# Sample attention over the paged cache: the maximum's chain, the register loads and the exponentials in another order

## The reference, cut to what matters

```python
ckv_past = cache_ckv[j][page_table].reshape(bs, -1, R_KV)      # 8 samples, 4096 rows of 256
kpe_past = cache_kpe[j][page_table].reshape(bs, -1, D_ROPE)    # 8 samples, 4096 rows of 32
sp = (einsum('bqhr,bkr->bhqk', ql, ckv_past) + einsum('bqhd,bkd->bhqk', qp, kpe_past)) * MLA_SCALE
p = softmax(concatenate([sp, s], axis=-1), axis=-1)            # s: the score of the new token itself
o = einsum('bhqk,bkr->bqhr', p[..., :n_past], ckv_past) + einsum('bhqk,bkr->bqhr', p[..., n_past:], ckv)
```

## Time and profile before

| | |
|---|---|
| median of three runs | 3507.61 us |
| the profiled execution | 3497.2 us, its span 3495.1 us |
| busy share of the span | TensorE matmul 85%, VectorE 62%, ScalarE 41%, GpSimd 37% |
| granted TensorE clock, mean | 0.961 |
| sample attention | 1930.4 to 2145.2 us from the span's start |

### The profile page before, as it was taken

One profiled execution on the slowest core, in us unless ns is written; L12 is line 12 of the kernel. 1 busy time (PEld: TensorE's weight loads), 2 busy tenths in 40 slices (PEclk: granted clock), 3 DMA queues, 4 the chain that ended last, 5 costly groups with the idle time before them and its releaser, 6 DMA issues. The chain is left out here.

```text
span 3495.1 us, 34133 instructions
## 1 busy us (share of the span) xinstructions
PE 2962.2 (85%) x10273; PEld 1451.8 (42%) x10273; DVE 2162.7 (62%) x5228; ACT 1420.9 (41%) x4150; POOL 1301.0 (37%) x1112
## 2 busy tenths in 40 slices
PE   8987888888888888887999876888888888888887
PEld 7643333433434433432554544433333444433332
DVE  4873667666677766664262223666766676866765
ACT  3121445444444544443352122444444444543444
POOL 0211544444544444442001010454444444444442
PEclk9988999999999999999999798999999999999999
DMA  4015999999999999998203586999999999999998
GB/s 163 20 61 219 419 422 414 421 421 417 418 407 421 414 421 421 420 419 348 102 1 163 182 313 246 418 421 421 417 422 420 416 407 421 406 421 421 421 421 360
DMA packets 197093, 1213.48 MB, mean 347 GB/s; under 512 B 24527, under 2 KB 46959, under 8 KB 56869
## 3 DMA queue, kind: packets, MB, share of 16 engines
q0 software_dynamic: 154368, 1128.34, 77.9%
q1 hardware_dynamic: 41245, 82.06, 6.5%
q10 hardware_dynamic: 1296, 0.90, 0.1%
HBM read 1207.23 MB, written 4.46 MB: 347 GB/s over the span
## 5 line engine op out<-in xcount | busy, mean ns | idle before, releaser
L1581 PE MATMUL p_acc<-p_rows,p_diag 128*128 128x512 f32 (+1 forms) x4160 | 1976.1, 617 | 406.6 <-ACT p_diag L1184 404.8
L1096 POOL DMA_INDIRECT p_rows<-in_peer_uv,p_ids x1024 | 1217.6, 1189 | 1383.5 <-PE p_acc L1581 1279.5
L1414 DVE CUSTOM_DVE_ANT_0 p_rows<-p_rows,p_x_n 128x1024 f32<-128x1024 f32 x1024 | 1244.5, 1224 | 787.3 <-DMA p_rows<-in_peer_uv,p_ids 784.6
L1581 PEld LDWEIGHTS p_acc<-p_rows,p_diag 128*128 128x128 f32 (+1 forms) x4160 | 755.6, 193 | 1502.7 <-ACT p_diag L1184 780.3
L1178 ACT ACTIVATE p_acts<-p_dots 128x1 f32<-128x1 f32 x1040 | 208.3, 200 | 866.1 <-DVE p_dots L1414 864.1
L1184 ACT ACTIVATE p_diag<-ident,p_gated 128x128 f32<-128x128 f32 x1024 | 411.1, 401 | 33.5
L1180 ACT ACTIVATE p_gated<-p_acts,p_gates 128x1 f32<-128x1 f32 x1024 | 301.6, 295 | 33.2
L1531 PE MATMUL p_q_bank<-p_w_q,p_xT 128*128 128x256 f32 x1024 | 236.2, 384 | 2.2 <-ACT p_xT L1127 2.2
L1531 PEld LDWEIGHTS p_q_bank<-p_w_q,p_xT 128*128 128x128 f32 x1024 | 197.0, 193 | 55.9 <-issue 28.5
L1150 ACT COPY p_q_rows<-p_q_bank 128x256 f32<-128x256 f32 x68 | 25.2, 371 | 353.2 <-PE p_q_bank L1531 353.2
L1623 POOL DMA_INDIRECT smp_past<-in_cache_rows,smp_row_ids x32 | 30.1, 940 | 367.1 <-PE c_ps L2103 228.7
(11 more groups left out here) (408 smaller groups left out, 2489.2 us busy)
## 6 DMA issues: line engine op xcount, KB each, us to landing
d_turned_c<-in_cache_turned SPq DMA_DIRECT2D x128, 144.0 KB
p_w_q<-in_w_q_heads SPq DMA_DIRECT2D x16, 1024.0 KB, 12.8
p_rows<-in_peer_uv,p_ids POOLq DMA_INDIRECT x1024, 13.5
a_w_in<-in_ab_w_in SPq DMA_DIRECT2D x6, 1024.0 KB
a_w_in<-in_ab_w_out SPq DMA_DIRECT2D x1, 4096.0 KB
c_arena<-in_c_w_out SPq DMA_DIRECT2D x1, 4096.0 KB, 12.6
smp_past<-in_c_w_out SPq DMA_DIRECT2D x1, 4096.0 KB
a_w_in<-in_ab_w_in SPq DMA_DIRECT2D x4, 1008.0 KB, 21.0
```

What stands on the lines that cost most here:

```text
L1096: nc.gpsimd.indirect_dma_start(out=rows[:, slot % RING, :], out_offset=None, in_=w[f"peer_uv{layer}"], in_offset=bass.IndirectOffsetOnAxis ...
L1414: nc.vector.tensor_tensor_reduce(rows[:, k % RING, 0:D_MODEL], rows[:, k % RING, 0:D_MODEL], x, 1.0, 0.0, ALU.mult, ALU.add, dots[:, slot ...
L1581: last = nc.tensor.matmul(acc[done % 2][0:n, at], diag[:, slot // GROUP % 4, j, 0:n], rows[:, (slot + j) % RING, D_MODEL + 512 * b:D_MODEL ...
```

## The change

Four edits, all in `latent_sample`:

1. `load_turned` fills all eight registers of a piece first, then waits for `s_ps`, then issues the eight DMAs.
2. The exponential over 1024 scores becomes two over 512 each, each with its own signal and its own column of sums (three columns instead of two); the waits on `e_ready` count halves.
3. TensorE: `fold_heads(b - 2)` goes ahead of group 0, `turn_max(b - 1)` ahead of group 1, `spread_max(b - 1)` ahead of groups 2 and 3.
4. ScalarE: `exps(b - 1)` goes ahead of the copy of group 2. VectorE: `largest(b - 1)` goes ahead of the copy of group 1.

```diff
@@ load_turned (SyncE)
+                starts = [nc.sync.value_load(smp["turned_ids"][0:1, at:at + 1], min_val=0, max_val=w["cache_turned"].shape[0] - 128)
+                          for at in range(KEYS_8 * piece, KEYS_8 * piece + KEYS_8)]
                 if piece >= TURNED_BUFS:
                     sp.wait_ge(s_ps, 2 * ((piece - TURNED_BUFS) // 2 + 1))
-                for k in range(KEYS_8):
-                    at = KEYS_8 * piece + k
-                    row = nc.sync.value_load(smp["turned_ids"][0:1, at:at + 1], min_val=0, max_val=w["cache_turned"].shape[0] - 128)
+                for k, row in enumerate(starts):
                     sp.dma_start(turned_c[:, piece % TURNED_BUFS, k, :], w["cache_turned"][bass.ds(row, 128), :]).then_inc(turned_in[piece % TURNED_BUFS], 16)
@@ exps (ScalarE)
-                nc.scalar.activation(sc[:], s_bank[:, :], ACT.Exp, bias=nbias[:], scale=MLA_SCALE, accum_out=sums[:, 0:1]).then_inc(e_ready, 1)
-                nc.scalar.activation(self_e[:, 0:B], self_s[:, b, :], ACT.Exp, bias=nbias[:], scale=MLA_SCALE, accum_out=sums[:, 1:2]).then_inc(self_e_ready, 1)
+                for half in range(2):
+                    at = slice(KEYS * half, KEYS * half + KEYS)
+                    nc.scalar.activation(sc[:, at], s_bank[:, at], ACT.Exp, bias=nbias[:], scale=MLA_SCALE, accum_out=sums[:, half:half + 1]).then_inc(e_ready, 1)
+                nc.scalar.activation(self_e[:, 0:B], self_s[:, b, :], ACT.Exp, bias=nbias[:], scale=MLA_SCALE, accum_out=sums[:, 2:3]).then_inc(self_e_ready, 1)
@@ order on ScalarE
-                page_out(b, 2)
                 if b:
                     exps(b - 1)
+                page_out(b, 2)
@@ order on VectorE
-                page_out(b, 1)
                 if b:
                     largest(b - 1)
+                page_out(b, 1)
@@ scores, turn_weights (TensorE)
-                    pe.wait_ge(e_ready, b)
+                    pe.wait_ge(e_ready, 2 * b - 1 + half)
-                pe.wait_ge(e_ready, b + 1)
                 for half in range(2):
+                    pe.wait_ge(e_ready, 2 * b + 1 + half)
@@ order on TensorE
+                if b >= 2:
+                    fold_heads(b - 2)
                 turn_pages(b, 0)
                 if b == 0:
                     latent_queries()
-                if b >= 2:
-                    fold_heads(b - 2)
-                turn_pages(b, 1)
...
                 if b:
                     turn_max(b - 1)
+                turn_pages(b, 1)
+                if b:
+                    spread_max(b - 1)
                 turn_pages(b, 2)
                 if b == 0:
                     self_scores()
                 turn_pages(b, 3)
-                if b:
-                    spread_max(b - 1)
                 scores(b, 0)
```

More of the change, by code:

```diff
@@ L2209, in latent_sample @@
         nbias = sb("nbias", [128, 1])
-        sums = sb("sums", [128, 2])
+        sums = sb("sums", [128, 3])
         total = sb("total", [128, 1])
@@ L2220, in latent_sample @@
         o_bank = ctx.enter_context(nc.psum_tensor("d_o", [128, 2 * R_KV], F32))
-        m1_row, bias_col, total_cols = m_bank[0:1, 0:128], m_bank[:, 128:129], m_bank[:, 132:134]
+        m1_row, bias_col, total_cols = m_bank[0:1, 0:128], m_bank[:, 128:129], m_bank[:, 132:135]
         fold_out, self_turned = m_bank[:, 192:192 + 2 * H_C], m_bank[:, 256:384]
```

## The result

The changed kernel takes 3477.5 us, the median of six runs (3476.34 to 3484.32). The kernel before took 3507.28 us in its six (3504.94 to 3509.02). The profiled execution of the changed kernel took 3477.95 us, its span is 3475.9 us.

What follows compares the result with a forecast made beforehand. It took TensorE's waits in sample attention, chiefly for late turned-cache DMAs beside the gather, as the bound; -9.9 + 0.7 - 0.5 + 0.1 - 0.3 = -9.9 us off 3507.6 gave 3497.7 us, range 3487 to 3505.

Steps and rivals of the forecast that it cites:

- the mechanism: SyncE, turned loads: registers loaded before the scores end, eight issues in 4.1 us instead of 9.8, landed about when the gather begins.
- the price of the waits that go: TensorE before the turned half: waits of iterations 3 to 6 go, iteration 2's stays, 14.4 - 4.5 = 9.9 us saved.
- The base: Whole kernel: saving of 9.9 us taken off the median, 3507.6, though the profiled execution was 10.4 us below it.
- What is late next: Per sample, SyncE's 19.4 us and the DMA engines' 18.3 us both fit periods of about 21.5, by 2 to 3 us.
- rival B: Turned-cache wait stays in part, bursts moving slowly or meeting the gather: half remaining gives 3502.6 us, all 3507; chance 0.20.
- Iteration 2: Its turned-cache wait of 4.47 us stays, because SyncE is behind and issues piece 5 under the gather.
- Iteration 1: Scores start at 1967.5 against 1968.04, -0.5 us; piece 3 lands with a cover of 1 us.
- The term of +0.7: Edits 2 to 4, iterations 3 to 6: scores at +8.52 after the gather's start against +8.17, together +0.7 us.
- The held signal (R): TensorE's signal to ScalarE, next the bias, is held until 5.65 us after the gather's start.
- The halves: ScalarE: two exponentials of 512 scores take 2 x 0.59 = 1.18 us, fixed cost 0.07 each.
- A: More than forecast: register loads overlap or held signals come earlier, iteration 2 gains too; 3491, with all 3486 us; chance 0.20.
- C: Slower: TensorE idles longer ahead of the first half, 7.5 us, with slow clock, 12 us; +9.6, 3517 us; chance 0.06.

Runs made afterwards that it cites:

- The burst that starts with the gather: Kernel before with edit 1 alone, pieces from 5 on also waiting for the weighted sum that releases the gather: 3514.42 us, ratio 1.0024.
- the usual execution of before: The kernel before, unchanged, run and profiled once more: 3506.57 us, ratio 1.0001; its profiled execution took 3506.88 us.
- Edit 1 alone: The kernel before with only the new load_turned, eight registers loaded ahead of the wait: 3474.31 us, ratio 0.992.
- the constants: Kernel before with edit 1 alone, fixed rows in place of register loads (wrong keys, same bytes and DMAs): 3464.99 us, ratio 0.9879.
- issues given to GpSimd: Kernel before with edit 1 alone, GpSimd issuing piece 4 and half of each odd piece from 5 on: 3465.53 us, ratio 0.9883.

## Why the prediction was wrong, by its steps

**Edit 1: the mechanism held, its size did not.** What was forecast of SyncE is there. Seven gaps between the issues of piece 3 take 3.61 us, 0.52 each (forecast 0.51); eight loads take 4.4 us (from the last issue of a piece to the first of the next 4.93 us where nothing is waited for; forecast 4.7). That the seven DMAs of the earlier trace rows bear out 0.51 was a slip, though: from the first start to the last end there are six gaps, (3.79 - 0.34) / 6 = 0.575 us. And not every burst is issued within the 4.1 us forecast: pieces 5, 7 and 13 take 4.41, 5.18 and 4.87 us. In iterations 3 to 5 the eight issues still end ahead of the gather's first packets, and the wait is gone. The burst that starts with the gather shows that this is the cause. On that contention the Trainium skill, "DMA: Bandwidth & Descriptors" (Queues, rings and completion order), says that each engine takes its queues in turn, a packet at a time; the nearly equal packet counts of the earlier trace rows agree.

**The failed step is the price of the waits that go, 14.4 - 4.5 = 9.9 us.** It priced the wait of one execution and left the rest of the iteration as it stood in it, 21 to 22 us for iterations 3 to 6. Measured: 17.59 in 3 to 5, and 24.84 in 6. Of iteration 3's 24.1 us, 2.96 was the wait. Another 1.97 us was the late start of the scores (+8.17 against the usual +6.20), and 1.39 us the slow first half behind it (3.31 against 1.92 us). I took both as fixed. They were no part of the normal run: the delay is absent in the usual execution of before, and the slow half followed a wait. In the usual execution the four waits of iterations 3 to 6 are 26.2 us (7.03 + 6.66 + 5.10 + 7.42) and the slow turned halves behind them some 9.8 (3.64 against 1.92 us, and a longer rope part). Together that is the 36.0 us by which these four iterations are longer than four of iteration 7's length. The change took 28.2 of them: iteration 6 kept 7.3, and the four periods are each 0.13 us longer than before without a wait (17.59 against 17.46). Edit 1 alone, in its own trace, took 34.1. An upper bound stood in the rows: iteration 7 does the same work on TensorE in 17.5 us, so the four iterations had about 25 us to lose even in that execution (24.1 + 23.4 + 24.3 + 23.4 - 70). I didn't ask what kept them from it.

**The base.** I saw that the profiled execution was 10.4 us under the median and subtracted its difference from the median. That is right only if the 10 us lie outside the stage. They lay inside it, in the very waits that the change takes away: 225.5 against 214.8 us, with 35.0 against 14.4 us of waits for the turned cache.

**What is late next.** Forecast: SyncE's 19.4 us a sample fit into periods of 21.5. Measured: 17.7 to 18.6 us from one odd piece to the next (2001.63, 2019.97, 2037.62, 2056.24), a bit better, but the periods became 17.59. So SyncE falls behind, by up to a us per sample, until piece 13 meets its gather: 4.80 us of wait and the slow half behind it, 7.3 us. That is rival B's mechanism, in one iteration of four. The DMA engines, forecast at 18.3 us a sample, have hardly more room: in iteration 4 of the changed kernel their share is 1.04, at 397 GB/s, where it was 0.81 in iteration 3 before. A step that shortens a period has to be followed by a second look at everything that was to fit into it.

**Iteration 2** kept its wait, as forecast, and for the reason given; the wait is 8.88 us instead of 4.47, as it was before in the usual execution (8.81).

**Iteration 1.** Forecast a gain of 0.5 us, with a cover of 1 us for piece 3. Piece 3 is issued from 1962.37 to 1966.3, two us earlier than in the estimate, but iteration 0 now also ends 4.4 us earlier (1955.92 against 1960.28), and the wait for it is 2.40 us. Up to the end of iteration 1 nothing changed, 44.5 against 44.4 us.

**Edits 2 to 4.** The term of +0.7 was added up a little high even on its own rows: in iterations 5 and 6 the scores had started at +8.25 and +8.24 (2063.82 - 2055.57, 2088.09 - 2079.85) and in iteration 4 at +8.93, which against +8.52 makes +0.5. The held signal (R) was read out of one execution. None of the other traces of this study has it; the scores start at +6.34, 0.14 us later than in the usual execution before. Group 2's copy is the last release, as forecast. The halves cost more than the 0.07 us taken from the copies: two of them run from 2009.44 to 2010.78, 1.34 us against 1.11, so 0.23 us. The Trainium skill, "ScalarE: Activation LUTs" (Rules for kernel authors), with its 0.3 us for each ACTIVATE, was nearer than my row, which was of an instruction without a sum. Nothing hangs on it: with one exponential the time is the same. That these edits bring next to nothing was right, forecast at +0.7 - 0.5 + 0.1 - 0.3 and measured at no difference, with the DMA waits over them and with few left. The parts that no wait hides came out near: iteration 7 takes 17.59 against 17.46 us (forecast +0.1), and the rest behind it 29.0 against 29.2 (forecast -0.3).

**The rivals.** A named the register loads as the reason for iteration 2, which the constants bore out, and its "more" is the side on which the time fell; but that side was luck: its loads would have overlapped, and they don't, iteration 2 kept its wait, and its figures, 3491 and 3486, lie 8 us and more above the result. C, a longer idle with a slow clock, has nothing for it: the idle ahead of the first half is 1.25 us. It did name a price that the forecast left out, some 3 us of slow clock behind a long wait; it was already being paid.

Still open is what delayed the signals in the one profiled execution of before.

## What to carry to other kernels

Before pricing a wait, look whether the profiled execution is a usual one; if it lies off the median, profile the kernel again, since the difference may lie in the very stage that changes. Take as the upper bound the iteration that does the same work without the wait, here 17.5 us beside 24, clock and late starts included. Where two queues share the DMA engines, move the small packets ahead of the big ones, and once a period has shrunk, check again that the issuing engine's own cycle and the DMA engines' work still fit into it; if the first doesn't, give part of it to another engine.

## What the runs showed of the hardware

- A load of a register from SBUF on SyncE costs 0.55 us and doesn't overlap the next one (eight in 4.4 us); a DMA with its source row in a register is issued in 0.52 us. GpSimd issues the same DMA in 0.58 us with its registers loaded (eight in 4.67 us).
- With issues given to GpSimd the kernel is 9 us faster than with edit 1 alone (3465.53 against 3474.31), and SyncE is freed of them. The Trainium skill, "DMA: Bandwidth & Descriptors" (Rules for kernel authors), says of such spreading that it only saves the issuing engine's time. The kernel with constants agrees that this time was worth having, 9.3 us; no run here measures what spreading does to bandwidth.
- From 2007 to 2008, with one packet of the gather moved, SyncE's queue moved 0.27 MB. A burst started together with the gather's first instruction was waited for until 17.6 us after its start.
- TensorE's clock fell in long waits. In iterations 1 to 7 of all traces but the first of before, the turned half (where all its matmuls are recorded) took 3.45 to 3.64 us behind unbroken waits of 3.71 to 9.91 us, 3.08 behind 2.40 us, and 1.92 or 1.93 with no wait or one of up to 1.72 us. In the first profiled execution of before it took 1.92 behind waits of 1.8 to 3.0 us in iterations 3 to 6. There the slow clock had come and gone before, in the first half: in iteration 3 the granted clock was 0.50 from 2016.6 to 2019.9 and 1.00 from 2020 to 2027. The granted clock was 0.88 and 0.86 in the windows of iterations 2 and 6 of the changed kernel, which hold the long waits, and 1.00 in 3, 4, 5 and 7.
